# Two operand tensors of the matrix products, moved by some hundreds of bytes in SBUF

## What is computed

```python
for layer in range(2):                       # first block
    x = layer_norm(a * x + mixer(x) @ w_out)         # mLSTM + neighbourhood attention, then differential attention
    x = layer_norm(a * x + memory_cross_attention(x, mem, wq, wkv, wo))
    x = layer_norm(a * x + (silu(x @ w_gate) * (x @ w_up)) @ w_down)        # hidden width 2816
for l in range(2):                           # second block
    x = layer_norm_2(a * x + 0.5 * swiglu_ffn(x, ...))
    x = layer_norm_2(a * x + mixer_sublayer(x, ...))  # sparse + stick-breaking attention, convolution, gates
    x = layer_norm_2(a * x + memory_cross_attention_2(x, mem, ...))
    x = layer_norm_2(a * x + 0.5 * swiglu_ffn(x, ...))
```

## Time and profile before

| | |
|---|---|
| median of 3 runs | 2470.63 us (2469.42 to 2477.91) |
| the profiled execution: its time | 2475.34 us |
| its span, first to last instruction | 2473.5 us |
| mean granted TensorE clock | 0.966 |
| TensorE matmuls, busy | 2344.4 us, 95% |
| VectorE, ScalarE busy | 1470.3 us (59%), 1091.4 us (44%) |
| DMA | 412.59 MB, mean 167 GB/s |

### The profile page before, as it was taken

The page is one execution under the profiler, slowest core; times in us unless marked ns, Lnnn a source line. Parts: engine busy times, 40 slices in busy tenths (PEclk is TensorE's granted clock), DMA queues, the critical chain, the costliest instruction groups (busy, mean ns, idle before and its releaser), DMA issues. The chain is left out here.

```text
span 2473.5 us, 38184 instructions
## 1 busy us (share of the span) xinstructions
PE 2344.4 (95%) x16097; PEld 2138.9 (86%) x16097; DVE 1470.3 (59%) x1648; ACT 1091.4 (44%) x1238; POOL 126.6 (5%) x178
## 2 busy tenths in 40 slices
PE   8989999998999999999999998999999999998998
PEld 7868899877888988988887987998998987896996
DVE  6466555478756555554765676556555655676554
ACT  3444444344444434432555444434443365444442
POOL 2140000000000000000011000000000012000000
PEclk9899999999999999997999999999998899999999
DMA  8535355553545555555442563655555443464653
GB/s 255 162 94 196 125 190 188 187 161 103 188 136 185 191 187 187 189 187 165 138 135 81 187 228 120 196 187 183 194 190 185 136 128 114 129 217 134 203 189 118
DMA packets 329402, 412.59 MB, mean 167 GB/s; under 512 B 15189, under 2 KB 261137, under 8 KB 329105
## 3 DMA queue, kind: packets, MB, share of 16 engines
q1 hardware_dynamic: 320160, 377.71, 47.0%
q0 software_dynamic: 9072, 32.44, 4.3%
HBM read 405.13 MB, written 4.98 MB: 166 GB/s over the span
## 5 line engine op out<-in xcount | busy, mean ns | idle before, releaser
L1365 DVE TENSOR_TENSOR wl<-raw,wh 128x2048 fp32r<-128x2048 f32 (+2 forms) x379 | 827.5, 2188 | 708.1 <-ACT wh L955 622.8
L324 PE MATMUL bank<-xl,wh 128*128 128x256 f32 x3440 | 976.1, 284 | 10.4 <-issue 9.7
L324 PE MATMUL bank<-xh,wl 128*128 128x256 f32 x3440 | 966.5, 281 | 0.0
L324 PE MATMUL bank<-xh,wh 128*128 128x256 f32 x3440 | 965.7, 281 | 0.0
L955 ACT ACTIVATE wh<-raw 128x2048 fp32r<-128x2048 f32 (+2 forms) x379 | 688.8, 1820 | 449.7 <-PE bank L324 428.6
L324 PEld LDWEIGHTS bank<-xl,wh 128*128 128x128 f32 x3440 | 660.5, 192 | 25.0 <-issue 24.2
L324 PEld LDWEIGHTS bank<-xh,wh 128*128 128x128 f32 x3440 | 661.6, 192 | 0.0
L324 PEld LDWEIGHTS bank<-xh,wl 128*128 128x128 f32 x3440 | 660.3, 192 | 1.0 <-issue 0.2
L324 PE MATMUL bank<-wl,hh 128*128 128x512 f32 x528 | 205.9, 390 | 0.0
L324 PE MATMUL bank<-wh,hh 128*128 128x512 f32 x528 | 205.5, 389 | 0.0
L324 PE MATMUL bank<-wh,hl 128*128 128x512 f32 x528 | 205.4, 389 | 0.0
(11 more groups left out here) (305 smaller groups left out, 2774.5 us busy)
## 6 DMA issues: line engine op xcount, KB each, us to landing
raw<-in_ffn_w_in SPq DMA_DIRECT2D x88, 1024.0 KB, 5.1
raw<-in_w_mix_in SPq DMA_DIRECT2D x56, 1024.0 KB, 5.3
raw<-in_ffn_w_gu SPq DMA_DIRECT2D x44, 1024.0 KB, 5.1
raw<-in_ffn_w_out SPq DMA_DIRECT2D x40, 1024.0 KB, 5.1
raw<-in_ffn_w_down SPq DMA_DIRECT2D x20, 1024.0 KB, 5.1
raw<-in_mem_wkv SPq DMA_DIRECT2D x16, 1024.0 KB, 5.8
raw<-in_even_w_in SPq DMA_DIRECT2D x14, 1024.0 KB, 6.4
raw<-in_odd_w_in SPq DMA_DIRECT2D x12, 1024.0 KB, 5.2
```

The lines of the kernel that those rows point to most:

```text
L324: ins = pe.transpose(o, a, b) if transpose else pe.matmul(o, a, b, start=start, stop=stop)
L1365: dve.tensor_tensor(wl[:, t % PARTS, 0:nk * w], raw_tile(t), wh[:, t % PARTS, 0:nk * w].bitcast(F32), ALU.subtract)\
```

## The change

The two tensors change order and places; `xl` now lies below `xh`. `x`, `z` and all from `gap_oh` upward keep their places.

```diff
     x = sb("x", [P, TB, D])
     z = sb("z", [P, TB, D])
-    sb("gap_xh", [P, 112])
+    sb("gap_xl", [P, 32])
+    xl = sb("xl", [P, KC, S], F32R)
+    sb("gap_xh", [P, 32])
     xh = sb("xh", [P, KC, S], F32R)
-    xl = sb("xl", [P, KC, S], F32R)
-    sb("gap_oh", [P, 16])
+    sb("gap_oh", [P, 64])
     st = ExitStack()
     btab = sb("btab", [P, 8, 512], F32, st)
```

## The result

The changed kernel takes 2497.6 us (median of 4 runs, 2486.9 to 2500.0), the kernel before 2471.1 us (4 runs): 1.0094 times as long, 95% interval 1.0058 to 1.0129. A second measurement with more runs (experiment 9) gave 1.0065 (1.0042 to 1.0087); one of its twelve runs, 2657.9 us at a mean granted clock of 0.832, is in a slower state of the chip and is left out. It is slower, by 0.65 to 0.94% as the two medians have it; I had forecast no change.

A forecast was written before the change was run, and what follows sets the result against it. The prediction took TensorE's matmul count times spacing to bound the kernel. With writes and stationary use at 0 and half the slow share gone (6 us), 2475.3 became 2469 us, no change that can be told; range 2433 to 2515.

The forecast's parts named there:

- R1: Moving `xh`, `xl`: weight load and moving read collide at the new distance; all slow 2508 us, one step worse 2553; chance 0.35.
- What bounds the kernel: Whole kernel: TensorE, busy 2344.4 of 2473.5 us; 10,320 of 16,097 matmuls have `xh` or `xl` moving, with almost no idle time before them.
- Two paces of the same code at the same address: Six FFNs: identical matmuls spaced 113.3 or 117.7 ns, each held for a whole stretch, independent of clock and DMA.
- the bounds: The 10,320 matmuls: all fast 12.5 us less, all slow 33 more; below the fast pace 57 less, above the slow 78 more.
- R2: Moving `xh`, `xl`: a collision at distance 64 today goes away; 2418 us for all, 2433 for two of three products; chance 0.21.
- the 42 us: Estimated gain on the 10,320 matmuls at 4.1 ns each, by the skill's issue gap, beside 12.5 us for the slower pace.
- R3: Matmul streams: only the slow pace vanishes, 12.5 us less, 2463 us; chance 0.12.
- R4: Matmul streams: the address plays no part, same mix of paces as before, 2469 to 2478 us; chance 0.16.
- Writes: 56 ScalarE copies and 56 VectorE subtractions writing the two tensors: taken as 0, at worst 3.6 us.
- Stationary use: 288 matmuls of 512 columns with `xh` or `xl` stationary: taken as 0, at most 1.3 us either way.

The follow-up runs named there:

- experiment 9: The changed kernel again, word for word, with more runs, against the kernel before: 2490.3 us (11 runs) against 2472.0 (23 runs).
- experiment 10: Bare matmul streams, not the whole kernel; part one moved `wl` and `xl` together: 117.0 to 120.8 ns when moved by 32 to 224 bytes.

## Why the prediction was wrong

The time lies inside the stated range of 2433 to 2515 us, in the part that belonged to R1, and 28 us above the value forecast.

**What bounds the kernel** was right: 10,320 matmuls without cover. A spacing higher by 3.35 ns is 34.6 us; 18 to 26 were measured, and of what is missing most is put down to the clock (experiment 9).

**Two paces of the same code at the same address** was read rightly, and so was their size: 113.3 and 117.7 ns in the prediction, 113.3 and 117.8 in the streams. That the timing of a stream's start picks between them fits the streams, where the number of transposes in front was all that differed.

**The step that failed** is the one that chose between the bounds: that the two paces "are not a property of the address alone", and that with more distance there was "no reason for the slow one to be commoner". The pace at the trace's one distance was taken for what any distance gives. The streams show 113.3 ns, with the low weights in their place, only at distance 192 (by 256 bytes), one pair of 64; in every other pair, in two or three starts each, the paces were 116.6 ns and up. For the pair of the changed kernel that made 117.75 ns of 114.4. The trace had a hint that I set aside: every 256-column stream in it, `mh` and `yh` too, lay at that distance, so it held no evidence on any other. In that case the bounds should have carried the forecast, not the mean of what was seen.

**R1** is nearest to what happened: about the second pace everywhere, by an effect of the distance on every stream. That the two reads collide is its reason, and it fits, since the spacing goes by the distance between the two addresses; no run shows the collision itself. Its price, 2508 us, was 10 us too high against 2497.6: 4 us because it was counted from the profiled execution (2475.3) and not from the median (2471.1); the other 6 go with the higher clock (0.972 on average in the four runs). The share of matmuls already at the second pace was near right (27% as estimated, 23% of the triples counted). Its point against itself, that 512-column streams stay near one pace, was weak: at the only distances of the trace, 0 and 64, they are at 226.7 and 228.9 ns, and at the others they are 5 to 8 ns above the lower of the two. **R2** fell: nothing under 113.3 ns in some 870 streams of 256 columns. The 109 ns in it leans on a row of transposes, 107 ns for 128 columns; by the start times most steps between transposes of `x` are 109 ns. That is twice the 53.3 ns of 128 columns at 2.4 GHz and a little more, and the "two passes" rest on this alone. The Trainium skill (TensorE: Matmul & The Clock Gate, "Back-to-back issue gap") gives N/2.4 + 2.5 ns for a single matmul taken by itself, and says that in a stream of weight loads and matmuls both set the spacing. So its 109.2 ns was no measure for these streams, and neither was the 42 us worked out from it. **R3** did not occur. **R4** fell: with nothing but addresses changed, the time rose beyond its interval in five kernels. The Trainium skill (SBUF — State Buffer, "Who interferes with whom") has two independent read ports for TensorE, one for the moving operand and one for the weight load. That the ports don't touch each other is not what these runs show for float32r: the spacing is 113.3 to 121 ns by the distance between what the two read, with no other engine at work. The measurement decides; what it is that they share isn't shown.

**The small terms.** Writes: 0, as taken. Stationary use: the triples of 512-column matmuls with `xh` or `xl` stationary went from 687.3 to 693.5 ns, 2 ns for each of 288, 0.6 us.

**What stays open:** which of the addresses must agree (part one of experiment 10 fell), whether the load or the output is what a smaller stationary piece relieves, and why the granted clock was higher in some of the layouts.

## What to carry to other kernels

Where TensorE streams float32r operands with a weight load for every matmul, the place of the tensors in SBUF is a parameter: count the matmuls in a window of a full-clock stream, and compare it with the columns over 2.4 GHz. If all streams of the trace lie at one distance from their weights, the trace says nothing of another; a kernel of bare streams at each distance tells all of them in one run, and its paces carried over to the whole kernel within 0.2 ns (the changed kernel lay between the two that its streams showed). A pace can depend on how a stream starts, so one stretch is not enough.

## What the runs showed that I had not expected

- At the full clock the pace of a 256-column float32r stream with a weight load for each matmul takes values from 113.3 to 121.8 ns, by the distances between the operands taken by 256 bytes; the absolute remainder played no part at the three distances where it was varied.
- At the lower clock the same streams are at 213.3 ns, 256 columns at 1.2 GHz, at every distance measured.
- At the full clock nothing ran under 113.3 ns, 6.6 ns above 256 columns at 2.4 GHz; 512 columns were at 226.7 ns at best. Both are 17/16 of the columns' time.
- At the best distance two paces exist, 113.3 and 117.8 ns; with the low weights 128 bytes further only the lower one came, in 20 starts of 20.
- Moving `xl` alone cost more (41 us) than moving both (18 to 26 us); moving `xh` alone cost 23 us.
